# Differential attention scores: from full fp32 matmuls on 32 rows to one fp32r pass on stacked parts that go through DRAM

## What is computed

```python
DA_HEADS = 8
DA_HEAD_DIM = BRANCH_W // (2 * DA_HEADS)        # 32
def diff_attention(q, k, v, lam, lam_init, subln):
    # q (B, L, H, 2, d), k (B, K, H, 2, d), v (B, K, H, 2d)
    scale = DA_HEAD_DIM ** -0.5
    def block(qb):
        s = jnp.einsum('qbhid,bkhid->bhiqk', qb, k).astype(jnp.float32) * scale
        p = jax.nn.softmax(s, axis=-1)
        a = (p[:, :, 0] - lam * p[:, :, 1]).astype(v.dtype)
        return jnp.einsum('bhqk,bkhd->qbhd', a, v)
    o = rmsnorm(map_query_blocks(block, q), subln) * (1 - lam_init)
# latent tokens: q and k turned by axial_rope, keys = own 512 + 128 cached context keys
# context tokens: no rope, their own 128 keys; k and v of the context are outputs too
```

## Time and profile before

| | us |
|---|---|
| median of 3 runs | 2908.49 (2906.88 to 2916.24) |
| the profiled execution, its own time | 2910.96 |
| span of that execution | 2909.2 |
| PE busy in the span | 2760.9 (95%) |
| DVE, ACT, POOL busy | 1878.3, 980.7, 1438.2 |
| mean granted TensorE clock | 0.974 |

### The profile page before, as it was taken

The page is one execution under the profiler, slowest core; times in us unless marked ns, Lnnn a source line. Parts: engine busy times, 40 slices in busy tenths (PEclk is TensorE's granted clock), DMA queues, the critical chain, the costliest instruction groups (busy, mean ns, idle before and its releaser), DMA issues.

```text
span 2909.2 us, 43789 instructions
## 1 busy us (share of the span) xinstructions
PE 2760.9 (95%) x17224; PEld 2483.7 (85%) x17224; DVE 1878.3 (65%) x2941; ACT 980.7 (34%) x1843; POOL 1438.2 (49%) x620
## 2 busy tenths in 40 slices
PE   7879899999999998999998989999999998999998
PEld 2348777888888998999997969797988898999998
DVE  6456577674445558888886478565544565855866
ACT  3442112315655115242242112313565213422422
POOL 0425233283433774656665605065434575667554
PEclk9879998999999999999999999899999999999999
DMA  5422243141111432334222216032111331222222
GB/s 224 140 98 90 87 138 131 70 123 39 52 53 46 162 101 95 118 93 124 80 88 83 88 65 229 12 129 85 53 46 45 124 126 59 80 86 75 88 80 80
DMA packets 80537, 275.34 MB, mean 95 GB/s; under 512 B 9003, under 2 KB 14763, under 8 KB 78156
## 3 DMA queue, kind: packets, MB, share of 16 engines
q1 hardware_dynamic: 48124, 168.77, 18.8%
q10 hardware_dynamic: 32208, 103.77, 10.3%
HBM read 248.91 MB, written 23.59 MB: 94 GB/s over the span
## 4 chain that ended last, share of the span: by engine, by line
PE 74%; DVE 12%; ACT 5%; DVEq 4%; DMA 3%; issue 2%; POOLq 0%; POOL 0%; ACTq 0%; SPq 0%
PE PS L606 32%; PE PS L946 9%; PE PS L1086 7%; PE PS L667 4%; PE PS L995 3%; PE PS L741 2%; DVEq L2108 2%; DMA wraw<-in_w_strips 2%; PE PS L893 2%; DVE bsum L2109 2%; PE PS L616 1%; PE PS L967 1%; PE PS L877 1%; PE PS L707 1%; PE PS L829 1%
## 5 line engine op out<-in xcount | busy, mean ns | idle before, releaser
L574 POOL TENSOR_SCALAR whi<-wraw 128x1024 fp32r<-128x1024 f32 x188 | 550.3, 2927 | 982.9 <-PE PS L606 485.7
L576 POOL TENSOR_TENSOR wlo<-wraw,whi 128x1024 fp32r<-128x1024 f32 x212 | 552.8, 2608 | 90.1 <-ACT whi L1375 60.9
L1673 DVE CUSTOM_DVE_ANT_0 adap<-ada,cond 128x1024 f32<-128x1024 f32 x176 | 315.9, 1795 | 32.6 <-DMA ada<-in_w_ada 11.8
L606 PE MATMUL PS<-hhi,whi 128*128 128x320 f32 x1152 | 264.4, 311 | 11.6 <-POOL wlo L576 11.3
L606 PE MATMUL PS<-hlo,whi 128*128 128x320 f32 x1152 | 262.9, 309 | 0.0
L606 PE MATMUL PS<-hhi,wlo 128*128 128x320 f32 x1152 | 262.7, 309 | 0.0
L587 POOL TENSOR_TENSOR blo<-bsum,bhi 128x512 fp32r<-128x512 f32 x120 | 175.9, 1472 | 168.0 <-ACT bhi L1538 168.0
L2067 DVE SCALAR_TENSOR_TENSOR x<-PS,mod,x 128x128 f32<-128x128 f32 (+2 forms) x240 | 90.8, 433 | 177.5 <-PE PS L606 174.9
L606 PEld LDWEIGHTS PS<-hhi,whi 128*128 128x128 f32 x1152 | 192.4, 188 | 14.4 <-POOL wlo L576 12.6
L1086 PE MATMUL PS<-hhi,bhi 128*128 128x320 f32 x640 | 199.3, 311 | 1.6 <-POOL blo L587 1.0
L1086 PE MATMUL PS<-hhi,blo 128*128 128x320 f32 x640 | 197.7, 309 | 0.0
(11 more groups left out here) (335 smaller groups left out, 7276.5 us busy)
## 6 DMA issues: line engine op xcount, KB each, us to landing
wraw<-in_w_strips SPq DMA_DIRECT2D x292, 512.0 KB, 3.6
ada<-in_w_ada ACTq DMA_DIRECT2D x80, 512.0 KB, 4.9
spectra<-hst ACTq DMA_DIRECT2D x48, 256.0 KB, 2.1
cond<-conds ACTq DMA_DIRECT2D x7, 1024.0 KB, 7.2
hld<-spectra ACTq DMA_DIRECT2D x8, 768.0 KB, 5.1
hld<-spectra ACTq DMA_DIRECT2D x12, 512.0 KB, 3.7
part<-hacc ACTq DMA_DIRECT2D x8, 640.0 KB, 3.5
macc<-part ACTq DMA_DIRECT2D x8, 640.0 KB, 4.2
```

What stands on the lines that cost most here:

```text
L574: nc.gpsimd.tensor_scalar(hi, raw, 1.0, None, ALU.mult)
L576: nc.gpsimd.tensor_tensor(lo, raw, hi, ALU.subtract).then_inc(w_split, 1)
L606: ins = pe.matmul(out[:, h, :], w[:, kt, :], mv[:, h * HALF:(h + 1) * HALF], start=start and m == 0, stop=stop and m == 2)
L1673: ins = V.tensor_tensor_reduce(adap[s][:, :], ada[s][j][:, :], cond[s][:, c, :], 1.0, 0.0, ALU.mult, ALU.add, mraw[:, 2 * m + c:2 * m + c ...
```

## The change

The queries and keys of the differential attention are split into a high fp32r part and the rest, and stacked along the rows of the array: for one head and one map, `dstq` holds the 32 high rows, the 32 low rows and both again, and `dstk` the 32 high rows twice and the 32 low rows twice. One fp32r pass over 128 rows then gives all four products. Since rows have to move between partitions, the parts go through a DRAM tensor `dqk`.

- ACT makes `dqhi` (`da_high`), DVE `dqlo` (`da_low`), six buffers each. SP sends the high parts out, between its strip loads, ACT the low ones (`da_low_out`), both to `dqk`.
- The cached keys are no longer spread by the host; they are split on the core (`dckhi`, `dcklo`) and sent out in eight transfers.
- `stack_in(h)` reads one head back, six transfers, doubled in the reading; two heads have buffers. Heads 0 and 1 are read before the loop, behind a wait of ACT for all writes, and ahead of modulation chunks 4 to 7. Heads 2 to 7 are read in the loop, one at the start of each head.
- The loop goes head by head, so a small unit is followed by four big ones.
- The new context keys go out in four transfers in place of one.

```diff
+        dqk = nc.dram_tensor("dqk", [DEPTH, 2, KB, 4, 2, 32, T + C], F32, kind="Internal").ap()
         def steps_before(n):
-            return 8 + min(4 * n, 32) + max(0, (312 * (min(n, 40) - 8)) // 32)
+            h, qb = divmod(min(n, 40), NT)
+            return 8 + 43 * h + (4 + 39 * (qb - 1) // 4 if qb else 0)
 # SP
             for n in range(3, DEPTH * STRIPS):
                 strip_load(n)
+                lay, i = divmod(n, STRIPS)
+                if S_DA + 3 <= i < S_DA + 11:
+                    i -= S_DA + 3
+                    sp.wait_ge(s_dhi, nth(lay, s_dhi, i + 2))
+                    sp.dma_start(dqk[lay, i // 4, i % 4, :, 0, :, 0:T], dqhi[i % 6][:, :].bitcast(F32)).then_inc(
+                        s_stk if i // 4 else s_stq, 16)
 # PE, da_scores
-                    qb, h = n // HEADS, n % HEADS
-                    pe.matmul(PS[:, 0, :], q1, dak[r1, ch, C:T], start=True, stop=True)
-                    pe.matmul(PS[:, 2, 0:384], q2, dak[r2, ch, C + 128:T], start=True, stop=True)
-                    pe.matmul(PS[:, 1, 384:512], q2, dak[r2, ch, C:C + 128], start=True, stop=True)
-                    pe.matmul(PS[:, 1, 0:128], q, k[:, 0:128], start=True, stop=True)
-                    pe.matmul(PS[:, 2, 384:512], q, k[:, 128:256], start=True, stop=True).then_inc(s_ds, 1)
+                    h, qb = divmod(n, NT)
+                    if qb == 0:
+                        pe.wait_ge(s_st[h % 2], nth(lay, s_st[h % 2], 96 * (h // 2 + 1)))
+                    for m in range(2):
+                        q, k = dstq[h % 2][m][:, qb * 128:qb * 128 + 128], dstk[h % 2][m]
+                        first = DA_COL + DA_MAP * m
+                        if qb == 0:
+                            ins = pe.matmul(PSF[:, first + L:first + L + C], q, k[:, 0:C], start=True, stop=True)
+                        else:
+                            border = 512 * (m + 1) - first
+                            for lo, hi in ((0, border), (border, L + 128)):
+                                ins = pe.matmul(PSF[:, first + lo:first + hi], q, k[:, C + lo:C + hi],
+                                                start=True, stop=True)
+                    ins.then_inc(s_ds, 1)
 # ACT
+                def da_high(n):
+                    act.wait_ge(s_drope, nth(lay, s_drope, n + 1))
+                    if n >= 6:
+                        act.wait_ge(s_stq, nth(lay, s_stq, 128))
+                    A(dqhi[n % 6][:, :], drot[n % 2][:, :], ACT.Copy).then_inc(s_dhi, 1)
+                    if n >= 4:
+                        act.dma_start(a["new_da_k"][lay, :, n - 4, :], drot[n % 2][:, 0:C]).then_inc(s_ko, 16)
+                def da_low_out(n):
+                    act.wait_ge(s_dlo, nth(lay, s_dlo, n + 2))
+                    act.dma_start(dqk[lay, n // 4, n % 4, :, 1, :, 0:T], dqlo[n % 6][:, :].bitcast(F32)).then_inc(
+                        s_stk if n // 4 else s_stq, 16)
+                def stack_in(h):
+                    c, hm = h // 2, 2 * (h % 2)
+                    for m in range(2):
+                        q = dqk[lay, 0, c, hm + m, :, :, 0:T].rearrange("g p n -> (g p) n")
+                        act.dma_start(dstq[h % 2][m][:, :].bitcast(F32), q.unsqueeze(0).broadcast_to(
+                            [2, 64, T])).then_inc(s_st[h % 2], 16)
+                        for g in range(2):
+                            k = dqk[lay, 1, c, hm + m, g, :, :]
+                            act.dma_start(dstk[h % 2][m][64 * g:64 * g + 64, :].bitcast(F32), k.unsqueeze(
+                                0).broadcast_to([2, 32, T + C])).then_inc(s_st[h % 2], 16)
+                for c in range(KB):
+                    for part2, src in enumerate((dckhi, dcklo)):
+                        act.dma_start(dqk[lay, 1, c, :, part2, :, T:T + C], src[:, c, :].bitcast(F32)).then_inc(s_stk, 16)
                 for n in range(8):
...
+                    if n >= 6:
+                        act.wait_ge(s_ko, nth(lay, s_ko, 16 * (n - 3)))
                     A(halves(draw[n % 2][:, :]), pair((n + 3) % 4), ACT.Copy,
...
+                    if n >= 1:
+                        da_high(n - 1)
+                    if n >= 2:
+                        da_low_out(n - 2)
+                act.wait_ge(s_stq, nth(lay, s_stq, 128))
+                act.wait_ge(s_stk, nth(lay, s_stk, 256))
+                for h in range(2):
+                    stack_in(h)
                 for k in range(4, KD):
                     ada_load(3, KD * lay + k, (lay, 2 * KD + k))
 # ACT, in the loop behind da_exp(n, 1)
+                    if n % NT == 0 and NT <= n < 35:
+                        stack_in(n // NT + 1)
 # DVE, behind the rope of n; and ahead of the loop
+                    if n >= 1:
+                        da_low(n - 1)
+                dve.wait_ge(s_stk, nth(lay, s_stk, 256))
```

More of the change, by code:

```diff
@@ L256, in build @@
         napt = [at(f"napt{i}", 144 + 2 * i, [128, 4, 128]) for i in range(2)]
-        daq = at("daq", 71, [128, KB, T])
-        dak = at("dak", 81, [128, KB, T])
+        dstq = [[at(f"dstq{i}{m}", 71 + 5 * i + 2.5 * m, [128, T], F32R) for m in range(2)] for i in range(2)]
+        dstk = [[at(f"dstk{i}{m}", (81, 84, 87, 123.5)[2 * i + m], [128, T + C], F32R) for m in range(2)]
+                for i in range(2)]
+        drot = [at(f"drot{i}", 91 + 2.5 * i, [128, T]) for i in range(2)]
+        dqhi = [at(f"dqhi{i}", k, [128, T], F32R) for i, k in enumerate((71, 73.5, 76, 78.5, 96, 98.5))]
+        dqlo = [at(f"dqlo{i}", k, [128, T], F32R) for i, k in enumerate((81, 83.5, 86, 88.5, 126.5, 129))]
+        dck = at("dck", 119.5, [128, KB, 128])
+        dcklo = at("dcklo", 119.5, [128, KB, 128], F32R)
+        dckhi = at("dckhi", 151.5, [128, KB, 128], F32R)
         yda_hi = at("yda_hi", 71, [128, KB, T], F32R)
@@ L378, in build @@
         s_noT = sem("na_and_da_out_turned")
-        s_nyhi = sem("yna_hi_done")
-        s_yna = sem("yna_done")
-        s_dq = sem("da_qk_sum")
+        s_nyhi = sem("yna_and_yda_hi_done")
+        s_yna = sem("yna_and_yda_done")
         s_dqe = sem("da_qk_raw")
         s_drope = sem("da_rope")
-        s_dv = sem("da_v_sum")
-        s_dve = sem("da_v_kept")
-        s_dcache = sem("da_cache_in")
+        s_dhi = sem("da_qk_hi")
+        s_dlo = sem("da_qk_lo")
+        s_stq = sem("da_queries_out")
+        s_stk = sem("da_keys_out")
+        s_st = [sem(f"da_stack_in{i}") for i in range(2)]
         s_lamv = sem("lambda_dots_and_da_square_sums")
@@ L1426, in _ @@
                         ada_load(3, KD * lay + n // 2, (lay, 2 * KD + n // 2))
+                    if n >= 1:
+                        da_high(n - 1)
+                    if n >= 2:
+                        da_low_out(n - 2)
+                da_high(7)
+                for n in (6, 7):
+                    da_low_out(n)
+                act.wait_ge(s_stq, nth(lay, s_stq, 128))
+                act.wait_ge(s_stk, nth(lay, s_stk, 256))
+                for h in range(2):
+                    stack_in(h)
                 for k in range(4, KD):
                     ada_load(3, KD * lay + k, (lay, 2 * KD + k))
-                act.wait_ge(s_drope, nth(lay, s_drope, 8))
-                act.dma_start(a["new_da_k"][lay], dak[:, :, 0:C]).then_inc(s_ko, 16)
-                act.wait_ge(s_dv, nth(lay, s_dv, 1))
+                act.wait_ge(s_ko, nth(lay, s_ko, 16 * 6))
+                act.wait_ge(s_nv, nth(lay, s_nv, 2))
                 for i in range(NT):
-                    A(dav[:, i, :], PS[:, i, :], ACT.Copy).then_inc(s_dve, 1)
-                act.wait_ge(s_dve, nth(lay, s_dve, 1))
+                    A(dav[:, i, :], PS[:, i, :], ACT.Copy).then_inc(s_nve, 1)
+                act.wait_ge(s_nve, nth(lay, s_nve, NT + 1))
                 act.dma_start(a["new_da_v"][lay], dav[:, 0, :]).then_inc(s_ko, 16)
                 def da_exp(n, m):
-                    lo, q = 0 if n // HEADS else 512, 2 * (n % 2) + m
+                    lo, q = 0 if n % NT else 512, 2 * (n % 2) + m
                     if m == 0:
@@ L1443, in da_exp @@
                     p = (dp1, dp2)[m][n % 2]
[L1444 removed]
+                    ins = A(p[:, lo:640], PSF[:, DA_COL + DA_MAP * m + lo:DA_COL + DA_MAP * m + 640], ACT.Exp,
                             bias=mx[:, q:q + 1], scale=-1.0, accum_out=sum2[:, 2 * n + m:2 * n + m + 1])
@@ L1452, in da_keep @@
                         act.wait_ge(s_dpv, nth(lay, s_dpv, n))
-                    lo = 0 if n // HEADS else 512
+                    lo = 0 if n % NT else 512
                     A(dpt[:, :, :].rearrange("p i n -> p (i n)")[:, lo:640], PSF[:, 1536 + lo:1536 + 640],
@@ L1500, in _ @@
                     A(yda_hi[:, :, qb * 128:(qb + 1) * 128], PS[:, qb % 4, :].rearrange("p (c n) -> p c n", c=KB),
-                      ACT.Copy).then_inc(s_dyhi, 1)
+                      ACT.Copy).then_inc(s_nyhi, 1)
                 early_out(3)
@@ L1958, in da_max @@
                 def da_max(n):
```

(8 more changed lines are left out.)

86 lines of the change are left out of this document (41 added, 45 removed).

## The result

The changed kernel takes 3217.06 us (median of 4 runs, 3209.54 to 3222.85), the kernel before beside it on the same chip 2912.34 (2906.88 to 2916.24). The ratio is 1.105, 95% interval 1.101 to 1.108: slower, and inside the predicted range. The profiled execution took 3222.85 us and has a span of 3221.0 us.

The account below looks back on a forecast made before the run. PE was taken to bound the loop, but narrow transfers would hide its saving: +96 us before the loop and +46 in it, +142 a layer, +284 for both on 2910.96, so 3190 us, range 3020 to 3320.

Parts of the forecast that it names:

- The shape: Transfers to and from `dqk`: served by no more engines than outer pieces, 4 for a write, 2 for a read.
- The scores: Loop, big units: 1280 fp32r columns take 0.60 us, saving 1.12 us a unit, 36 us a layer.
- Before the loop: Ahead of the first layer's loop: first maximum at 748 us in place of 651.7, +96 us.
- The sum: Before the loop: last write at about 654, two heads' reads 66.6 us, landing until 729, then DVE's 18.9 us.
- In the loop: Each layer's loop: 249 + 83 = 332 us in place of 286, +46 us.
- the wait I had named: Loop: PE waits for transfers at each new head from the third on.
- the forecast's own terms: Loop, each head fetched: reads 33.3 us, strips and merged tiles 5, issue and semaphore 5; 43.3 against PE's 31.1.
- the 10 us that I added: Loop: merged tiles queue behind the reads, adding 10 us to DVE's waits, 11.7 us already.
- The ends of this term: Loop: lower and upper ends of -3 and +79 us around the +46 a layer.
- The signs: Expected in the profile: PE idle tens of us before first scores, slow `dstq` landings, PE waits at heads, scores 0.6 us apart.
- the third sign: Reads: a `dstq` transfer lands 8 us or more after issue alone, tens of us in the row of twelve.
- The line between gain and loss: Ahead of the loop: the change pays if the first maximum is under 37 us late, wanting four engines or more.

Follow-up runs that it names:

- wide reads: Changed kernel with each doubled read made two plain copies, 12 a head in place of six, same bytes: 2959.21 us.
- widening them: Changed kernel with the DRAM tensor laid out part-major, each part's write one copy of 128 rows, reads still on two engines: 3166.56 us.
- two experiments: Changed kernel with the reads of heads 2 to 7 left out, 3017.83 us; kernel before with its loop going head by head, 2907.55 us.
- The spread run: Changed kernel with the next head's six doubled reads issued over four units (2, 1, 1, 2) instead of all at the first: 3139.01 us.
- both wide: Changed kernel with part-major writes of 128 rows and every doubled read as plain copies of 32 rows, 16 a head: 2938.35 us.
- those spread: Changed kernel with wide writes and wide reads, the next head's 16 reads issued four at a time over a head's first four units: 2879.06 us.
- one 2% faster than before: Changed kernel, writes and reads wide, issues spread, chunks 4 to 7 ahead of the reads, only head 0 fetched before the loop: 2858.79 us.

## Why the prediction was right

**The shape.** The step that decided it was that a transfer is served by no more engines than it has outer pieces. For the reads it holds to the digit: share 0.13, two of sixteen, and wide reads take the loss away. (The Trainium skill, "DMA: Bandwidth & Descriptors", section "Rules for kernel authors", gives this rule for a leading zero-stride broadcast; the window of 700 to 720 us agrees.) For the writes, four engines are not read off anywhere; that widening them brings 50 us is shown.

**The scores.** 0.58 us for the predicted 0.60, and 35.9 us a loop for the predicted 36. This saving is not visible in the changed kernel at all; it took two experiments to see it.

**Before the loop**, +96 predicted, and the first maximum came 97.4 us later in the first layer. 4.9 us of that were there before the change begins (`yna_hi`, 560.24 and 565.17). By "ahead" it is +92.4, and +88.1 in the second layer. The sum was better than its terms. The last write landed at 671.5, not 654: 12.6 us worse behind the same start, since ACT's draws waited up to 16 us for PE, whose strips were held, so the writes did not follow each other as closely as the sum had them. From the first read's issue to chunk 4 it took 65.4 us, not 75: an engine did 25.5 KB/us, near the upper end of 26, not 21.6. And from chunk 4 to the end of `mod` it took 12.0 us, not 18.9: a half chunk takes 1.23 us here, where the earlier trace rows has 3.21 and 1.83. The errors are +12.6, -10 and -7. That they leave only -4 is luck.

**In the loop**, +46 predicted, +61.4 and +60.8 measured. The step that was wrong in kind is "in the loop a wait of PE for transfers at each new head from the third on". No such wait is in the profile. ACT is held for 15 to 18 us at the issue of six reads, the exponentials come late, and PE waits for `dpt`. The spread run shows that the wait I had named lies just underneath, at 40.3 us a head. The heads from the second to the fifth start 43.8 to 44.6 us apart, for a forecast of 43.3, but that closeness is luck too: with the measured 25.5 KB/us in place of 21.6 the forecast's own terms give 28.3 + 5 + 5 = 38.3 us (an estimate), and the hold made up the difference. The next two heads take 58.5 and 49.5 us. Without the reads these six take 29.7 to 32.0 us, so the four are 13 to 15 us longer by the reads, the fifth 28.5 and the sixth 17.5.

In size the term is short by 15 us. Two things in it were mis-sized. PE's busy time is 244.4 us against 229.4 with the reads left out, a clock term that I did not have. And the waits for spilled sums are 32.2 us where the earlier trace rows had 11.7, twice the 10 us that I added; nearly all of it is the one wait of 28.9 us in the head of 58.5. The head of 49.5 has no such wait, only the longest hold, 18.2 us. What stands against them, the engines' higher rate, was not measured apart in the loop. The ends of this term were not worked out alike: -3 leaves out the 10 us of waits, and +79 holds some 15. Nothing hangs on it, as the result lies between.

**The signs.** PE was idle for 60.8 us ahead of the first scores, and the scores are 0.58 us apart, as forecast. How long a single narrow read takes to land, the third sign, the profile doesn't say.

**The line between gain and loss.** I had put it at a first maximum less than 37 us late, with four engines or more. With both wide it is 18 and 21 us late (by "ahead") and the kernel is yet 0.8% slower, so that line did not count ACT's time at the issues. With those spread the kernel is faster.

## What to carry to other kernels

Before a transfer is counted by its bytes, look at its outermost dimension on both sides: a doubling placed there put 1.44 MB a head on two of sixteen engines, and two plain copies cost half a microsecond more to issue. A transfer that is slow to land also holds the engine that issues the next ones, so on an engine that has work of its own, issue a few at a time and put what is needed first ahead of them. And a saving on the bounding engine, here 36 us a layer, is worth nothing until what feeds that engine is on time: the same score matmuls stood in a kernel 10% slower and in one 2% faster than before.

## What the runs showed of the hardware

- An issue on ACT's queue takes 0.5 us until three or four narrow reads are outstanding, and then the issues go no faster than the reads land: 13.8 us for three of them, 721 KB, at 51 GB/s. Plain reads of the same parts went out at 0.6 us each, 24 in a row.
- With two engines at work (share 0.13) 51 GB/s were moved, 25.5 KB/us for each, in rows of 2.5 to 3 KB.
- With 16 issues at a head's start, a gap of 2.45 us in PE was followed by 3 us at a granted clock of 0.56. With 12 issues the gap at the same place was 1.2 us and the clock stayed at 1.00; over the loop it was 0.93 and 0.99. What decides between the two was not tried.
- fp32r matmuls on 128 partitions kept the rate that the wide ones had: 1280 columns, in blocks of 384 and 256, took 0.58 us, where the earlier trace rows gives 0.60.
